# Interleaving the two token blocks in the matmul's stationary operands (xg, mixed, ff)

## The chip, the cores and the metric

The kernel runs on one core of one Trainium2 chip. The metric is the device time of one execution in microseconds (us), from the profiler's side of the device. Engines are named as in the profile: PE is TensorE (PEld is its weight load), DVE is VectorE, ACT is ScalarE, POOL is GpSimd, SP is SyncE. SP and ACT also issue DMAs (rows SPq and ACTq).

## The reference: one decoder layer

The layer has 256 tokens of width 2048, everything in float32. Cut to what matters:

```
h = rmsnorm(x, g_mix);  proj = h @ w_in            # all projections of two attentions and two gates
out_a = sparse attention with an indexer (top 64 keys); out_b = forgetting attention
mixed = sigmoid(gate_a) * (out_a @ w_o_a) + sigmoid(gate_b) * (out_b @ w_o_b)
x = x + mixed @ w_out
h = rmsnorm(x, g_ffn)
x = x + (silu(h @ w_ffn_gate) * (h @ w_ffn_up)) @ w_ffn_down      # width 5632
h = rmsnorm(x, g_ple)
x = x + sigmoid(h @ w_ple_gate) * (p @ w_ple_proj)
return rmsnorm(x, g_final)
```

## The kernel before

Every weight matrix is read once from HBM in chunks of 512 KB (128 partitions x 1024 float32) into `ws`, four slots in turn. ACT makes a rounded high part `hs` of each chunk (line 416), DVE the remainder `ls` (line 720). The activations are kept in high and low parts too, and a product is three matmuls: high x high, low x high, high x low.

Two forms of matmul stand in the program. In the first (lines 1165 and 1174) the weights are PE's stationary operand and the activations `hn` are streamed. In the second (`by_token`, lines 1275 and 1280) the activations are the stationary operand, a block of 128 rows (contraction) by 128 columns (tokens), and 512 columns of the weights are streamed. `pe.matmul(out, stationary, moving)` is the order of the arguments. A chunk holds two contraction tiles of 128 and is used for two blocks of tokens (b = 0: tokens 0 to 127, b = 1: tokens 128 to 255), so it takes eight matmuls with `hs` and four with `ls`. Which columns are the stationary block is said by `block_of(src, k, part, b)` (line 1264).

In the second half of the program, three products have activations that were made token by token and have to be turned first: `mixed` for w_out, `xg` for the FFN's gate and up matrices and for w_ple_gate, and `ff` for w_ffn_down. Turning 512 features of 256 tokens goes in four steps:

1. `turn_quads` (DVE, line 989): for each block b one transpose inside 32x32 squares, into `t_rows`;
2. `move_quads` (SP and ACT queues, line 224): sixteen DMAs, eight from each queue, carry squares between partitions, from `t_rows` into `t_cols`, with runs of 1 KB per partition;
3. ACT writes the high part from `t_cols` (`mixed_high` line 570, `new_high` line 598, `ff_hi` line 646);
4. DVE writes the low part (`mixed_low` line 994, `new_low` line 1023, `ff_low` line 1090).

Each engine works through its list in the written order and waits for semaphores. Of the 512-feature pieces, only the last of a stage is soon wanted: PE has started the next product with the earlier pieces and waits for `mix_ready` or `xg_ready` before it takes the last two chunks' tiles.

Of the kernel before, what the change touches and what calls it, by code (L numbers as in the profile page):

```python
# [3 lines left out]
F32 = mybir.dt.float32  # L4
F32R = mybir.dt.float32r
I32 = mybir.dt.int32
ALU = mybir.AluOpType
ACT = mybir.ActivationFunctionType
AX_X = mybir.AxisListType.X
ds = bass.ds  # L10

P = 128
D_MODEL, TOK, D_FF, D_PLE = 2048, 256, 5632, 256
# [4 lines left out]
KT = D_MODEL // P  # L18
KT_O = HA * HEAD // P
KT_FF = D_FF // P  # L20
# [52 lines left out]
QUAD = 32  # L73
QUADS = P // QUAD
# [38 lines left out]
def hybrid_layer(nc, c_rows, x, p, positions, g_mix, w_in, b_f, w_o_a, w_o_b, w_out, g_ffn, w_ffn_gate,  # L113
# [15 lines left out]
    def sb(name, kb, shape, dt=F32):  # L129
        return nc.alloc_sbuf_tensor_at(name, [P, *shape], dt, offset=base + int(kb * 1024))  # L130

    x_tok = sb("x_tok", 0, [2, D_MODEL])
    heads_o = sb("heads_o", 16, [KT, 2 * TOK], F32R)
    xg = sb("xg", 16, [2, KT, TOK], F32R)
    junk = sb("junk", 16, [2, D_MODEL])
    hn = sb("hn", 48, [KT, 2 * TOK], F32R)
    mixed = sb("mixed", 48, [2, KT, TOK], F32R)
    ff = sb("ff", 48, [2, KT_FF, TOK], F32R)
    gates = sb("gates", 80, [2, 2, D_MODEL])
    q_idx = sb("q_idx", 80, [KT_O, TOK])  # L140
    rope = sb("rope", 104, [4, 2 * TOK])
# [22 lines left out]
    mix_a = sb("mix_a", 188, [2, WIDE])  # L164
    silu_g = sb("silu_g", 188, [2, WIDE])
    sq = sb("sq", 188, [2, WIDE])
    t_cols = sb("t_cols", 184, [QUADS, 4, 2, QUAD])
    lg = sb("lg", 192, [CAT])
    pt = sb("pt", 193.5, [CAT])
    mask = sb("mask", 196.5, [CAT])  # L170
# [6 lines left out]
    k_st = sb("k_st", 200.5, [TOK])  # L177
    v_st = sb("v_st", 201.5, [2, P])
    p_cols = sb("p_cols", 192, [KT_PLE, 2 * TOK], F32R)
    t_rows = sb("t_rows", 196, [QUADS, 4, 2, QUAD])  # L180
    p_tok = sb("p_tok", 200, [2, D_PLE])
    ident = sb("ident", 202.5, [P])
    c_sum = sb("c_sum", 204, [TOK])
    gains = sb("gains", 205.5, [3 * KT])
# [25 lines left out]

    def by_tile(t):

        return t[:, :, :, :, :].rearrange("p a k b n -> p (k b) a n")

    def in_quads(t):

        return t.rearrange("p k (b a n) -> p (k b) a n", b=2, a=QUADS)

    def move_quads(eng, t, odd):

# [31 lines left out]
    merged, mix_s, mix_high, mix_ready = map(S, ("merged", "mix_s", "mix_high", "mix_ready"))  # L252
    x_new, x_sq, xg_high, xg_ready = map(S, ("x_new", "x_sq", "xg_high", "xg_ready"))
# [3 lines left out]
    ff_silu, ff_s, ff_high, ff_ready = map(S, ("ff_silu", "ff_s", "ff_high", "ff_ready"))  # L257
# [148 lines left out]
    def _(act):  # L406
# [37 lines left out]
        for t in range(KT // 2):  # L444
# [3 lines left out]
            for m in range(2):  # L448
                k = 2 * t + m
# [117 lines left out]

        def mixed_high(n):
            act.wait_ge(moved, 16 * MOVES * (T_MIX + n + 1))
            act.activation(in_quads(mixed[:, 0, 4 * n:4 * n + 4, :]), by_tile(t_cols), ACT.Copy).then_inc(mix_high, 1)  # L570

        act.wait_ge(gate_out, 2 * N_WIDE)
        for n in range(N_WIDE):
            cols = slice(WIDE * n, WIDE * (n + 1))
            if n == 0:
                split_chunks(C_WO + 4, 4)
            else:
                split_and_move(C_WO + 8 * n + 4, T_MIX + n - 1)
                mixed_high(n - 1)
            for gate in (1, 0):  # L580
                act.activation(gates[:, gate, :, cols], gates[:, gate, :, cols], ACT.Sigmoid).then_inc(gate_ready, 1)
            split_chunks(C_WO + 8 * n + 8, 4)
# [10 lines left out]
        def new_high(stage, n):  # L593

            act.wait_ge(moved, 16 * MOVES * ((T_X, T_PLE)[stage] + n + 1))
            for m in range(4):
                k = 4 * n + m
                act.activation(in_quads(xg[:, 0, k:k + 1, :]), by_tile(t_cols)[:, 2 * m:2 * m + 2], ACT.Copy,
                               scale=gains[:, KT * (stage + 1) + k:KT * (stage + 1) + k + 1]).then_inc(xg_high, 1)

        def root(stage):
# [3 lines left out]
        for n in range(N_WIDE):  # L605
            split_and_move(C_OUT + 8 * n + 4, T_MIX + N_WIDE - 1 + n)
            if n == 0:
                mixed_high(N_WIDE - 1)
                act.wait_ge(p_t, 1)
                act.activation(p_cols[:, :, 0:TOK], side[:, 2, :].rearrange("p (m n) -> p m n", m=2), ACT.Copy).then_inc(p_high, 1)  # L610
            else:
                squares(0, n - 1)
                new_high(0, n - 1)
            split_chunks(C_OUT + 8 * n + 8, 4)

        def ff_pair(i, step, first=False):

            u = U_FFN + 4 * step + i * 8
            c = step + i * 2
            split_high(u + 1, 0)  # L620
            split_high(u + 1, 1)
            move_quads(act, T_FF - 1 + c, 1)
            split_high(u + 1, 2)
            split_high(u + 1, 3)
            if first:
                squares(0, 3)
                new_high(0, 3)
                root(0)
            else:
                ff_hi(c - 1)  # L630
            for j in range(SLOTS):
                split_high(u + 2, j)
            if first:
                act.wait_ge(rms_ready, 1)
            for b in range(2):
                ins = act.activation(silu_g[:, b, :], acc[:, 2 + b, :], ACT.Silu, scale=rms[:, 0, 1, b:b + 1])
            ins.then_inc(ff_silu, 1)
            for j in range(SLOTS):
                split_high(u + 3, j)
            for j in range(SLOTS):  # L640
                split_high(u + 4, j)

        def ff_hi(c):

            act.wait_ge(moved, (c + T_FF + 1) * (16 * MOVES))
            act.activation(in_quads(ff[:, 0, ds(c * 4, 4), :]), by_tile(t_cols), ACT.Copy).then_inc(ff_high, 1)

        ff_pair(0, 0, first=True)
        with act.Fori(0, (N_FFN - 1) // 2) as i:
# [3 lines left out]
        for n in range(N_WIDE):  # L653
            at = C_DOWN + FF_CH * n
            split_and_move(at + 4, T_PLE - 1 + n)
            if n == 0:
                ff_hi(N_FFN - 1)
            else:
                squares(1, n - 1)
                new_high(1, n - 1)  # L660
            split_chunks(at + 8, FF_CH - 4)
# [24 lines left out]
        n = N_WIDE - 1  # L686
# [27 lines left out]
    def _(dve):  # L714
# [54 lines left out]
        for t in range(KT // 2):  # L769
# [3 lines left out]
            for m in range(2):  # L773
                k = 2 * t + m
# [125 lines left out]
        for i in range(4):  # L900
# [6 lines left out]
            if i % 2 == 1:  # L907
                n = i // 2
# [77 lines left out]
        def turn_quads(rows, at):  # L986

            for b in range(2):
                dve.transpose(t_rows[:, :, :, b, :].rearrange("p q k n -> p k q n"),
                              rows[:, b, at:at + WIDE].rearrange("p (k q n) -> p k q n", k=4, q=QUADS)).then_inc(turned, 1)  # L990

        def mixed_low(n):
            dve.wait_ge(mix_high, n + 1)
            dve.tensor_tensor(in_quads(mixed[:, 1, 4 * n:4 * n + 4, :]), by_tile(t_cols),  # L994
                              in_quads(mixed[:, 0, 4 * n:4 * n + 4, :].bitcast(F32)), ALU.subtract).then_inc(mix_ready, 1)

        for n in range(N_WIDE):
            cols = slice(WIDE * n, WIDE * (n + 1))
# [17 lines left out]
        def new_low(stage, n):  # L1016

            for m in range(4):
                k = 4 * n + m
                dve.wait_ge(xg_high, KT * stage + k // 2 * 2 + 2)  # L1020
                gain = gains[:, KT * (stage + 1) + k:KT * (stage + 1) + k + 1]
                for b in range(2):
                    ins = dve.scalar_tensor_tensor(in_quads(xg[:, 1, k:k + 1, :])[:, b], by_tile(t_cols)[:, 2 * m + b], gain,  # L1023
                                                   in_quads(xg[:, 0, k:k + 1, :].bitcast(F32))[:, b], ALU.mult, ALU.subtract)
                ins.then_inc(xg_ready, 1)

        def new_x(stage, n, pair):

            cols = slice(WIDE * n, WIDE * (n + 1))
            dve.tensor_tensor(x_tok[:, :, cols], acc[:, 2 * pair:2 * pair + 2, :], x_tok[:, :, cols], ALU.add).then_inc(x_new, 1)  # L1030
            dve.wait_ge(x_new, 4 * stage + n + 1)
            turn_quads(x_tok, WIDE * n)
# [22 lines left out]
        def ff_pair(i, step, first=False):  # L1055
# [5 lines left out]
            if first:  # L1061
                new_low(0, 3)
                row_sums(0)
                inverse(0)
                dve.wait_ge(rms_ready, 1)
            else:
                ff_low(c - 1)
# [15 lines left out]
            ins.then_inc(ff_s, 1)  # L1083
            dve.wait_ge(ff_s, c + 1)
            turn_quads(ff_tok, 0)

        def ff_low(c):

            dve.wait_ge(ff_high, c + 1)
            dve.tensor_tensor(in_quads(ff[:, 1, ds(c * 4, 4), :]), by_tile(t_cols),  # L1090
                              in_quads(ff[:, 0, ds(c * 4, 4), :].bitcast(F32)), ALU.subtract).then_inc(ff_ready, 1)

        ff_pair(0, 0, first=True)
        with dve.Fori(0, (N_FFN - 1) // 2) as i:
# [37 lines left out]
        n = N_WIDE - 1  # L1132
# [19 lines left out]
    def _(pe):  # L1152
# [105 lines left out]
        with pe.Fori(0, 4) as i:  # L1258
            for e in range(2):
                n = e + i * 2  # L1260
# [3 lines left out]
        def block_of(src, k, part, b):  # L1264

            if src is hn or src is heads_o or src is p_cols:
                return src[:, k, part * TOK + b * P:part * TOK + (b + 1) * P]
            return src[:, part, k, b * P:(b + 1) * P]

        def by_token(at, slot, tiles, src, banks, first, last, width=WIDE):  # L1270

# [100 lines left out]
        for n in range(N_WIDE):  # L1372
# [5 lines left out]
            for c in range(K_CH):  # L1378
                k = (KT_O + KW * c) % KT
# [112 lines left out]
```

## Time and profile before

| | |
|---|---|
| median of 3 executions | 1490.59 us (1490.31 to 1490.77) |
| the profiled execution's own time | 1490.77 us |
| its span, first to last instruction | 1489.0 us |
| PE busy | 1459.5 us, 98% |
| PE weight loads busy | 1222.0 us, 82% |
| DVE busy | 884.0 us, 59% |
| ACT busy | 690.6 us, 46% |
| POOL busy | 49.9 us, 3% |
| mean granted clock of PE | 0.997 of full speed |
| chain that ended last | PE 94%, DVE 3%, DMA 1% |

The rows further down are of a few views: the page of the profile, the list of waits, the list of instruction groups by line, the timeline (start, duration, engine, line, tile written <- tiles read, and in brackets the idle time before it with what ended it), and the chain that ended last. A matmul's record is longer than the distance to the next one, since matmuls are pipelined: the pace is read from the starts.

### The profile page before, as it was taken

Reading aid. Unit: us, or ns where it says so; the run is one execution under the profiler, and the core shown is the slowest. Engines: PE = TensorE matmul, PEld = TensorE weight load, DVE = VectorE, ACT = ScalarE, POOL = GpSimd, SP = SyncE. Lnnn points to the kernel's source line nnn. Section 1 sums busy time; section 2 is a strip of 40 time slices with the busy share of each in tenths; the row PEclk is TensorE's granted clock in tenths of the full one; section 3 lists DMA queues with packets and bytes.
Section 4 is the critical chain, followed back from the end, with each engine's and each line's share of the span. In section 5 each row is a group of like instructions: output and inputs, shape, how many; then the busy total and the mean of one; then the engine's idle time right before and its main releaser. Section 6 shows DMA issues by size and latency. Waiting matters only on the chain.

```text
span 1489.0 us, 19456 instructions
## 1 busy us (share of the span) xinstructions
PE 1459.5 (98%) x6841; PEld 1222.0 (82%) x6841; DVE 884.0 (59%) x1066; ACT 690.6 (46%) x846; POOL 49.9 (3%) x80
## 2 busy tenths in 40 slices
PE   5999999999999999999999999999999999999996
PEld 5888888888888888887888888888888888888885
DVE  6966776667655576665555555455555455554654
ACT  5644445544444455445444444444444343443544
POOL 0021001100111000000000000000000000000000
PEclk9999999999999999999999999999999999999998
DMA  6666565556655577666666666766666766666663
GB/s 193 178 204 169 160 222 170 169 170 190 183 166 167 163 236 232 211 208 214 205 209 210 202 191 205 212 207 210 205 204 184 221 204 197 210 190 209 213 215 109
DMA packets 182574, 290.91 MB, mean 195 GB/s; under 512 B 18745, under 2 KB 67825, under 8 KB 182001
## 3 DMA queue, kind: packets, MB, share of 16 engines
q1 hardware_dynamic: 172944, 281.02, 61.8%
q10 hardware_dynamic: 9568, 9.07, 2.1%
q8 instruction: 39, 0.64, 0.2%
q14 instruction: 23, 0.18, 0.0%
HBM read 275.87 MB, written 2.11 MB: 187 GB/s over the span
## 4 chain that ended last, share of the span: by engine, by line
PE 94%; DVE 3%; DMA 1%; ACT 1%; ACTq 1%; issue 0%; DVEq 0%
PE acc L1275 50%; PE acc L1280 25%; PE acc L1165 8%; PE acc L1174 4%; PE side L1275 2%; PE side L1280 1%; DVE ls L720 1%; ACTq L224 1%; DMA rope_c<-in_rope_rows 1%; PE side L1321 0%; DVE hn L775 0%; PE side L1327 0%; DMA t_cols<-t_rows 0%; ACT hs L416 0%; PE side L1335 0%
## 5 line engine op out<-in xcount | busy, mean ns | idle before, releaser
L720 DVE TENSOR_TENSOR ls<-ws,hs 128x1024 fp32r<-128x1024 f32 (+1 forms) x520 | 629.9, 1224 | 535.7 <-ACT hs L416 531.3
L416 ACT ACTIVATE hs<-ws 128x1024 fp32r<-128x1024 f32 (+1 forms) x520 | 544.1, 1056 | 717.8 <-PE acc L1280 505.0
L1275 PE MATMUL acc<-hs,xg 128*128 128x512 f32 x1648 | 407.1, 389 | 1.1 <-DVE xg L1023 1.1
L1275 PEld LDWEIGHTS acc<-hs,xg 128*128 128x128 f32 x1648 | 309.3, 188 | 65.6 <-DVE xg L1023 1.5
L1280 PE MATMUL acc<-ls,xg 128*128 128x512 f32 x824 | 220.2, 389 | 0.0
L1280 PEld LDWEIGHTS acc<-ls,xg 128*128 128x128 f32 x824 | 154.7, 188 | 32.1
L1275 PE MATMUL acc<-hs,ff 128*128 128x512 f32 x704 | 173.8, 389 | 0.0
L1275 PE MATMUL acc<-hs,hn 128*128 128x512 f32 (+1 forms) x704 | 171.9, 387 | 0.0
L1275 PEld LDWEIGHTS acc<-hs,ff 128*128 128x128 f32 x704 | 132.2, 188 | 27.4
L1275 PEld LDWEIGHTS acc<-hs,hn 128*128 128x128 f32 x704 | 127.1, 188 | 24.2
L1165 PE MATMUL acc<-hn,hs 128*128 128x512 f32 x560 | 139.2, 393 | 0.0
L1165 PEld LDWEIGHTS acc<-hn,hs 128*128 128x128 f32 x560 | 101.5, 189 | 18.9
L1280 PE MATMUL acc<-ls,ff 128*128 128x512 f32 x352 | 94.1, 389 | 0.0
L1280 PE MATMUL acc<-ls,hn 128*128 128x512 f32 (+1 forms) x352 | 90.4, 380 | 0.0
L1174 PEld LDWEIGHTS acc<-hn,ls 128*128 128x128 f32 x560 | 74.3, 191 | 5.1 <-DVE hn L775 0.7
L1280 PEld LDWEIGHTS acc<-ls,ff 128*128 128x128 f32 x352 | 66.1, 188 | 13.7
L1174 PE MATMUL acc<-hn,ls 128*128 128x256 f32 x560 | 75.9, 283 | 0.5 <-DVE hn L775 0.5
L1280 PEld LDWEIGHTS acc<-ls,hn 128*128 128x128 f32 x352 | 64.2, 188 | 13.1
L1275 PE MATMUL acc<-hs,mixed 128*128 128x512 f32 x256 | 63.5, 390 | 0.5 <-DVE mixed L994 0.5
L1275 PEld LDWEIGHTS acc<-hs,mixed 128*128 128x128 f32 x256 | 47.9, 188 | 10.9 <-DVE mixed L994 1.0
L533 ACT ACTIVATE lg<-lg,neg_max 128x128 f32<-128x128 f32 (+1 forms) x32 | 14.3, 448 | 47.0 <-DVE neg_max L935 47.0
L1280 PE MATMUL acc<-ls,mixed 128*128 128x512 f32 x128 | 34.2, 389 | 0.0
(192 smaller groups left out, 815.2 us busy)
## 6 DMA issues: line engine op xcount, KB each, us to landing
ws<-in_w_in SPq DMA_DIRECT2D x152, 512.0 KB, 3.9
ws<-in_w_ffn_gate SPq DMA_DIRECT2D x88, 512.0 KB, 4.4
ws<-in_w_ffn_up SPq DMA_DIRECT2D x88, 512.0 KB, 4.4
ws<-in_w_ffn_down SPq DMA_DIRECT2D x88, 512.0 KB, 4.3
ws<-in_w_out SPq DMA_DIRECT2D x32, 512.0 KB, 4.7
ws<-in_w_ple_gate SPq DMA_DIRECT2D x32, 512.0 KB, 3.9
ws<-in_w_o_b SPq DMA_DIRECT2D x16, 512.0 KB, 4.6
ws<-in_w_o_a SPq DMA_DIRECT2D x16, 512.0 KB, 4.6
```

The lines of the kernel that those rows point to most:

```text
L224: eng.dma_start(t_cols[QUAD * q:QUAD * (q + 1), a, :, :, :], t_rows[QUAD * a:QUAD * (a + 1), q, :, :, :]).then_inc(moved, 16)
L416: act.activation(hs[:, j, 0:n], ws[:, j, 0:n], ACT.Copy).then_inc(h_split, 1)
L533: act.activation(lg[:, cols], lg[:, cols], ACT.Exp, bias=neg_max[:, b:b + 1], accum_out=sums[:, b:b + 1]).then_inc(exp_done, 1)
L720: dve.tensor_tensor(ls[:, j, 0:n], ws[:, j, 0:n], hs[:, j, 0:n].bitcast(F32), ALU.subtract).then_inc(l_split, 1)
L1165: mm = pe.matmul(acc_of(bank + m, 2 * TOK), hs[:, j, at], src[:, k, :], start=first and q == 0, stop=last and q == len(tiles) - 1)
L1174: mm = pe.matmul(acc_of(bank + m, TOK), ls[:, j, at], src[:, k, 0:TOK], start=False, stop=False)
L1275: pe.matmul(banks[b], block_of(src, k, part, b), hs[:, slot, q * width:(q + 1) * width], start=first and q == 0 and part == 0, stop=False)
L1280: mm = pe.matmul(banks[b], block_of(src, k, 0, b), ls[:, slot, q * width:(q + 1) * width], start=False, stop=last and q == len(tiles) - 1)
```

## The change

The two token blocks are no longer one behind the other in the columns of `xg`, `mixed` and `ff`, but interleaved: column 2j holds token j, column 2j + 1 token 128 + j. To that end the transposes write `t_rows` with a step of two elements, `t_cols` has the block as its innermost index, ACT and DVE copy runs of 64 elements where they copied runs of 32, and the stationary block of a matmul is read with a step of two elements (8 bytes) where it was read in one run. `xg`'s low part, which took two DVE instructions per tile of 128 features, takes one. `hn`, `heads_o` and `p_cols` keep their layout.

```diff
-    xg = sb("xg", 16, [2, KT, TOK], F32R)
+    xg = sb("xg", 16, [KT, 2 * TOK], F32R)
     (mixed and ff likewise)
-    t_cols = sb("t_cols", 184, [QUADS, 4, 2, QUAD])
+    t_cols = sb("t_cols", 184, [QUADS, 4, QUAD, 2])
     (t_rows likewise)
     def by_tile(t):
-        return t[:, :, :, :, :].rearrange("p a k b n -> p (k b) a n")
+        return t[:, :, :, :, :].rearrange("p a k n b -> p k a (n b)")
     def in_quads(t):
-        return t.rearrange("p k (b a n) -> p (k b) a n", b=2, a=QUADS)
+        return t.rearrange("p k (a n) -> p k a n", a=QUADS)
     turn_quads:
             for b in range(2):
-                dve.transpose(t_rows[:, :, :, b, :].rearrange("p q k n -> p k q n"),
+                dve.transpose(t_rows[:, :, :, :, b].rearrange("p q k n -> p k q n"),
     new_high (mixed_high and ff_hi likewise):
-                act.activation(in_quads(xg[:, 0, k:k + 1, :]), by_tile(t_cols)[:, 2 * m:2 * m + 2], ACT.Copy,
+                act.activation(in_quads(xg[:, k:k + 1, 0:TOK]), by_tile(t_cols)[:, m:m + 1], ACT.Copy,
     new_low:
-                gain = gains[:, KT * (stage + 1) + k:KT * (stage + 1) + k + 1]
-                for b in range(2):
-                    ins = dve.scalar_tensor_tensor(in_quads(xg[:, 1, k:k + 1, :])[:, b], by_tile(t_cols)[:, 2 * m + b], gain,
-                                                   in_quads(xg[:, 0, k:k + 1, :].bitcast(F32))[:, b], ALU.mult, ALU.subtract)
-                ins.then_inc(xg_ready, 1)
+                dve.scalar_tensor_tensor(in_quads(xg[:, k:k + 1, TOK:2 * TOK]), by_tile(t_cols)[:, m:m + 1],
+                                         gains[:, KT * (stage + 1) + k:KT * (stage + 1) + k + 1],
+                                         in_quads(xg[:, k:k + 1, 0:TOK].bitcast(F32)), ALU.mult, ALU.subtract).then_inc(xg_ready, 1)
     block_of:
-            return src[:, part, k, b * P:(b + 1) * P]
+            return src[:, k, part * TOK:(part + 1) * TOK].rearrange("p (n b) -> p b n", b=2)[:, b, :]
```

On DVE, between the last piece of w_out's product and the FFN, stood in a row before (`x_tok` is the residual in token order, `xg` the turned and scaled one):

```order
L1030 TENSOR_TENSOR x_tok<-acc,x_tok 128x2x512
L989 STREAM_TRANSPOSE t_rows<-x_tok 128x4x4x32 x2
L720 TENSOR_TENSOR ls<-ws,hs 128x1024 x4
L1023 SCALAR_TENSOR_TENSOR xg<-t_cols,gains,xg 128x128 x8
L1036 TENSOR_REDUCE sum_sq<-parts_sq 128x2
L1040 RECIPROCAL rms<-rms 128x2
L720 TENSOR_TENSOR ls<-ws,hs 128x1024 x12
```

And now, at the same place of the same engine:

```order
L1028 TENSOR_TENSOR x_tok<-acc,x_tok 128x2x512
L989 STREAM_TRANSPOSE t_rows<-x_tok 128x4x4x32 x2
L720 TENSOR_TENSOR ls<-ws,hs 128x1024 x4
L1021 SCALAR_TENSOR_TENSOR xg<-t_cols,gains,xg 128x256 x4
L1034 TENSOR_REDUCE sum_sq<-parts_sq 128x2
L1038 RECIPROCAL rms<-rms 128x2
L720 TENSOR_TENSOR ls<-ws,hs 128x1024 x12
```

Eight instructions of 128 elements became four of 256; nothing else has another place. This stands eight times in the program. At the hand-over of `mixed` to w_out's product, the same engine's list shows another shape only:

```order
 L720 TENSOR_TENSOR ls<-ws,hs 128x1024 x4
-L994 TENSOR_TENSOR mixed<-t_cols,mixed 128x1024
+L994 TENSOR_TENSOR mixed<-t_cols,mixed 128x4x256
 L720 TENSOR_TENSOR ls<-ws,hs 128x1024 x4
 L1008 TENSOR_TENSOR mix_b<-acc,gates 128x1024
```

The number of elements is the same; what was one row of 1024 in eight parts is four parts of 256. PE, SP and POOL have the same instructions in the same order.

## Rows read from the trace of the kernel before

**Rows 1.** The page: busy time by engine, and the granted clock in 40 slices.
```profile
PE 1459.5 (98%) x6841; PEld 1222.0 (82%) x6841; DVE 884.0 (59%) x1066; ACT 690.6 (46%) x846; POOL 49.9 (3%) x80
PEclk9999999999999999999999999999999999999998
```

**Rows 2.** List of waits of PE: us in total, times, longest.
```profile
PE acc L1275 <- DVE xg L1023: 1.1, 1, 1.1
PE acc L1275 <- DVE mixed L994: 0.5, 1, 0.5
```

**Rows 3.** Groups by line: count | busy us, mean ns | idle before.
```profile
L1275 PE MATMUL acc<-hs,xg 128*128 128x512 f32 x1648 | 407.1, 389 | 1.1 <-DVE xg L1023 1.1
L1280 PE MATMUL acc<-ls,xg 128*128 128x512 f32 x824 | 220.2, 389 | 0.0
L1275 PE MATMUL acc<-hs,ff 128*128 128x512 f32 x704 | 173.8, 389 | 0.0
L1275 PE MATMUL acc<-hs,mixed 128*128 128x512 f32 x256 | 63.5, 390 | 0.5 <-DVE mixed L994 0.5
```

**Rows 4.** Timeline, FFN: one matmul and the load that begins beside it.
```profile
1100.09 0.39 PE L1275 MATMUL acc<-hs,xg 128*128 128x512 f32 x1
1100.10 0.19 PEld L1275 LDWEIGHTS acc<-hs,xg 128*128 128x128 f32 x1
```

**Rows 5.** The chain that ended last: start, us, what (pieces of 8 and 16).
```profile
1061.04 1.81 PE acc L1275 x8
1063.76 1.81 PE acc L1275 x8
368.05 1.91 PE acc L1174 x16
```

**Rows 6.** Timeline, attention: matmuls of 128 columns, two passes each.
```profile
240.03 0.38 PE L1334 MATMUL side<-pt,v_st 128*128 128x128 f32 x2
240.25 0.39 PE L1335 MATMUL side<-pt,v_st 128*128 128x128 f32 x2
```

**Rows 7.** Groups by line: two POOL copies of one shape.
```profile
L388 POOL COPY q_st<-q_cols 128x256 f32 x16 | 18.0, 1124 | 87.1 <-DVE k_cols L959 73.8 <-DVE k_cols L728 12.4
L389 POOL COPY k_st<-k_cols 128x256 f32 x16 | 7.3, 458 | 0.0
```

**Rows 8.** Groups by line: DVE work on chunks, and around the turning.
```profile
L720 DVE TENSOR_TENSOR ls<-ws,hs 128x1024 fp32r<-128x1024 f32 (+1 forms) x520 | 629.9, 1224 | 535.7 <-ACT hs L416 531.3 <-DVE sel L881 1.4 <-DVE q_idx L842 0.3
L1090 DVE TENSOR_TENSOR ff<-t_cols,ff 128x1024 f32 (+1 forms) x11 | 13.4, 1219 | 0.0
L989 DVE STREAM_TRANSPOSE t_rows<-x_tok 128x512 f32<-128x512 f32 x16 | 10.4, 691 | 0.3
L1023 DVE SCALAR_TENSOR_TENSOR xg<-t_cols,gains,xg 128x128 fp32r<-128x128 f32 x64 | 17.5, 348 | 8.3 <-ACT xg L598 8.3
L775 DVE SCALAR_TENSOR_TENSOR hn<-acc,gains,hn 128x256 fp32r<-128x256 f32 x8 | 3.4, 479 | 1.1 <-ACT hn L450 1.1
```

**Rows 9.** Timeline, the last piece of `mixed` on its way to PE.
```profile
577.43 1.31 DVE L989 STREAM_TRANSPOSE t_rows<-mix_b 128x512 f32<-128x512 f32 x2
578.77 5.30 ACTq L224 DMA_DIRECT2D t_cols<-t_rows  x8
587.54 1.22 DVE L994 TENSOR_TENSOR mixed<-t_cols,mixed 128x1024 fp32r<-128x1024 f32 x1
588.81 2.12 PE L1275 MATMUL acc<-hs,mixed 128*128 128x512 f32 x8 [0.55 <-DVE mixed L994]
```

**Rows 10.** Timeline, the last piece of `xg` on its way into the FFN.
```profile
663.42 1.31 DVE L989 STREAM_TRANSPOSE t_rows<-x_tok 128x512 f32<-128x512 f32 x2
665.40 6.16 ACTq L224 DMA_DIRECT2D t_cols<-t_rows  x8
676.03 2.19 DVE L1023 SCALAR_TENSOR_TENSOR xg<-t_cols,gains,xg 128x128 fp32r<-128x128 f32 x8 [0.92 <-ACT xg L598]
677.23 2.11 PE L1275 MATMUL acc<-hs,xg 128*128 128x512 f32 x8 [1.07 <-DVE xg L1023]
```

**Rows 11.** Timeline, the last piece of `xg` before w_ple_gate.
```profile
1394.99 2.19 DVE L1023 SCALAR_TENSOR_TENSOR xg<-t_cols,gains,xg 128x128 fp32r<-128x128 f32 x8 [1.31 <-ACT xg L598]
1398.16 1.98 PE L1275 MATMUL acc<-hs,xg 128*128 128x512 f32 x8
```

More of the change, by code:

```diff
@@ L133, in hybrid_layer @@
     heads_o = sb("heads_o", 16, [KT, 2 * TOK], F32R)
-    xg = sb("xg", 16, [2, KT, TOK], F32R)
+    xg = sb("xg", 16, [KT, 2 * TOK], F32R)
     junk = sb("junk", 16, [2, D_MODEL])
     hn = sb("hn", 48, [KT, 2 * TOK], F32R)
-    mixed = sb("mixed", 48, [2, KT, TOK], F32R)
-    ff = sb("ff", 48, [2, KT_FF, TOK], F32R)
+    mixed = sb("mixed", 48, [KT, 2 * TOK], F32R)
+    ff = sb("ff", 48, [KT_FF, 2 * TOK], F32R)
     gates = sb("gates", 80, [2, 2, D_MODEL])
@@ L179, in hybrid_layer @@
     p_cols = sb("p_cols", 192, [KT_PLE, 2 * TOK], F32R)
-    t_rows = sb("t_rows", 196, [QUADS, 4, 2, QUAD])
+    t_rows = sb("t_rows", 196, [QUADS, 4, QUAD, 2])
     p_tok = sb("p_tok", 200, [2, D_PLE])
@@ L569, in mixed_high @@
             act.wait_ge(moved, 16 * MOVES * (T_MIX + n + 1))
-            act.activation(in_quads(mixed[:, 0, 4 * n:4 * n + 4, :]), by_tile(t_cols), ACT.Copy).then_inc(mix_high, 1)
+            act.activation(in_quads(mixed[:, 4 * n:4 * n + 4, 0:TOK]), by_tile(t_cols), ACT.Copy).then_inc(mix_high, 1)
         act.wait_ge(gate_out, 2 * N_WIDE)
@@ L645, in ff_hi @@
             act.wait_ge(moved, (c + T_FF + 1) * (16 * MOVES))
-            act.activation(in_quads(ff[:, 0, ds(c * 4, 4), :]), by_tile(t_cols), ACT.Copy).then_inc(ff_high, 1)
+            act.activation(in_quads(ff[:, ds(c * 4, 4), 0:TOK]), by_tile(t_cols), ACT.Copy).then_inc(ff_high, 1)
         ff_pair(0, 0, first=True)
@@ L993, in mixed_low @@
             dve.wait_ge(mix_high, n + 1)
-            dve.tensor_tensor(in_quads(mixed[:, 1, 4 * n:4 * n + 4, :]), by_tile(t_cols),
-                              in_quads(mixed[:, 0, 4 * n:4 * n + 4, :].bitcast(F32)), ALU.subtract).then_inc(mix_ready, 1)
+            dve.tensor_tensor(in_quads(mixed[:, 4 * n:4 * n + 4, TOK:2 * TOK]), by_tile(t_cols),
+                              in_quads(mixed[:, 4 * n:4 * n + 4, 0:TOK].bitcast(F32)), ALU.subtract).then_inc(mix_ready, 1)
         for n in range(N_WIDE):
@@ L1089, in ff_low @@
             dve.wait_ge(ff_high, c + 1)
-            dve.tensor_tensor(in_quads(ff[:, 1, ds(c * 4, 4), :]), by_tile(t_cols),
-                              in_quads(ff[:, 0, ds(c * 4, 4), :].bitcast(F32)), ALU.subtract).then_inc(ff_ready, 1)
+            dve.tensor_tensor(in_quads(ff[:, ds(c * 4, 4), TOK:2 * TOK]), by_tile(t_cols),
+                              in_quads(ff[:, ds(c * 4, 4), 0:TOK].bitcast(F32)), ALU.subtract).then_inc(ff_ready, 1)
         ff_pair(0, 0, first=True)
```

## The prediction

> **What bounds the kernel now.** Read the page first: PE is busy 98% of the span, and the clock row stands at 9 to the last slice but one: the clock granted is the upper level, 2.4 GHz [rows 1]. DVE works 59% and ACT 46% of the span, so neither is short of time on the whole. The list of waits comes next. In the part of the program that the change touches PE waits twice in all, 1.1 us for `xg` and 0.5 us for `mixed` [rows 2]; everywhere else it goes from one matmul to the next. So the time is the number of matmuls times their pace, plus two short stalls, and the change can move the end in three ways only: by the pace of PE, by those two stalls, or by making a hand-over late that is in time now.
>
> How many matmuls read the changed layout: with `hs`, 1648 on xg, 704 on ff and 256 on mixed; with `ls` half as many each (824, 352, 128) [rows 3]; and 24 in the closing chunks by the code (2 blocks x 2 chunks x 2 tiles x 3). That is 2608 + 1304 + 24 = 3936 of PE's 6841.
>
> Their pace is read in the chain: two pieces of eight begin 2.72 us apart with a piece of four (line 1280) between them, so twelve matmuls take 2.72 us, 226.7 ns each [rows 5]. The streaming of 512 columns at 2.4 GHz is 213.3 ns of that. 3936 x 226.7 ns = 892 us: 60% of the time hangs on this one number.
>
> **PE: the stationary block is read with a step of two.** No instruction is added or taken away on PE. What differs is how a weight load reads its 128 columns: every second float32 instead of a run. The question is how much of the load is hidden now. One load begins together with the matmul before it, at 1100.10 beside 1100.09 [rows 4], and its matmul begins one pace later, so it has 226.7 ns. How long it needs at least is seen where the stream is short: the four passes of lines 1334 and 1335 with 128 columns begin 0.22 us apart for two, 110 ns per load and matmul, though 128 columns at 2.4 GHz are 53 ns [rows 6]; there the load sets the pace. With 256 columns the pace is 1.91 / 16 = 119 ns [rows 5]. The load's record of 190 ns is thus longer than its share of the pace; some 80 ns of it run beside the next load. A load needs 110 ns and has 227: it may take 2.06 times as long before the pace changes at all.
>
> No instruction of this trace reads a stationary block with a step, so the price has to be bounded. Lower end: nothing, and not below nothing, because the load is hidden already (what could be gained beyond is a rival below). Upper end: the widest spread that I find in this trace between two instructions of one shape is that of two POOL copies, 1124 against 458 ns, 2.45 times [rows 7]. A load that were 2.45 times as long would take 270 ns; the pace would go from 226.7 to 270, and 3936 x 43.3 ns = 170 us. I take nothing: it needs more than a doubling to be seen, and the nearest rows on patterns say that breaking a row up is free: DVE's reads and writes in runs of 32 elements take 1219 ns where the plain chunk takes 1224 [rows 8].
>
> The page "SBUF — State Buffer" of the Trainium skill (section Specifications) bears on this: memory lines of 16 bytes, and full bandwidth as long as at least two accesses fall into one line. A step of 8 bytes gives exactly two. By that rule the load stays at its present length; the trace before has no load with a step, so it neither agrees nor disagrees.
>
> **DVE: the transposes write with a step of two.** There are 46, of 691 ns each [rows 8]. They run while DVE has nothing urgent, except where the last piece of a stage is on its way to PE. For `mixed` the chain is transposes (577.43), the eight DMA issues on ACT's queue (578.77, 5.30 us), ACT's two chunks and its high part, DVE's low part (587.54), PE after 0.55 us of waiting [rows 9]. For `xg` into the FFN it is the same from 663.42 to PE's wait of 1.07 us at 677.23 [rows 10]. There each ns that two transposes take longer comes out at the end. In the third place, before w_ple_gate, the low part of the tiles that PE wants first is written by 1394.99 + 3 x 0.26 + 0.35 = 1396.1 and PE takes it at 1398.16: 2 us of slack [rows 11]. The other pieces are wanted many chunks later. Behind the transposes in DVE's list stand the `ls` chunks, for which PE has a lead: DVE idles 535.7 us before them in all, waiting for ACT [rows 8].
>
> Price: lower end nothing (the engine takes one element at a time, and the same number of them); upper end again 2.45 times, 691 x 1.45 = 1.0 us per transpose, two at each of two places, 4.0 us. I take nothing, by the same nearest rows.
>
> The page "Vector Engine (DVE) Microarchitecture Reference" (section Measured stream behaviour on trn2) speaks against the change here: it says that a DVE port keeps its full rate only while it finds at least two neighbouring words of 4 bytes together, and that a destination which jumps at every element takes 1.71 ns (2.5 for small steps) per column where 1.05 is normal. An estimate from it is 512 x 0.66 to 512 x 1.45 ns, 0.34 to 0.74 us per transpose, and 1.4 to 3.0 us for the two places. The row of 691 ns is of writes in runs and can't decide it.
>
> **DVE: one instruction for two in `xg`'s low part.** 64 of 128 elements become 32 of 256. Eight of the short ones take 2.19 us, the last 0.35 of it, so they follow at 0.26 us; the tiles that PE waits for are ready after four: 676.03 + 3 x 0.26 + 0.35 = 677.16, and PE starts at 677.23 [rows 10]. The nearest rows for the long form are those on `hn`, 479 ns, eight in 3.4 us or 0.425 each [rows 8]: two are ready after 0.425 + 0.48 = 0.90 us, at 676.93. That takes 0.25 us off PE's wait of 1.07; what is late next is ACT's high part, which ended a little before 676.03. At the other seven places the gain lies beside other work. Bounds: 0 to 0.5 us.
>
> **ACT's copies and DVE's other low parts** keep their element counts, with runs of 64 for runs of 32: nothing, from 1219 against 1224 ns [rows 8]. The DMAs still carry 1 KB runs, the same number in the same places.
>
> **The sum**, against the profiled execution's 1490.77 us (span 1489.0 and 1.8 around it): 0 for PE's loads, 0 for the transposes, - 0.25 for the low part of `xg`, so 1490.5. That execution was 0.2 above the median, so I forecast 1490.3 for a median. What a measurement of this kernel tells from no change is about 0.2%, 3.0 us.
>
> **The rivals.**
>
> *The load gets longer than its cover* (slower). Place: every one of the 3936 matmuls. It decides from 227 ns for a load, about twice the present 110. If the step just doubles the load to 220 ns and the 13 ns between the pace of 226.7 and the stream of 213.3 have to be paid on top, the pace is 233 and the cost 3936 x 6.6 ns = 26 us: 1516. At 2.45 times it is 170 us: 1661. For it: nobody in this trace reads with a step, and the product has 60% of the time under it, so that a small excess is multiplied at once. Against it: 117 ns of cover. Chances 5% for the first and 8% for the second.
>
> *The transposes slow down* (slower, small). Two at each of two hand-overs, decisive from the first ns. At 2.45 times + 4.0 us: 1494.3. With less, say half again, + 1.4 us: 1491.7. Chance of anything over 0.5 us 15%; in a third of that it is beyond 0.2%, which is 5%.
>
> *PE gets faster* (faster by over 0.2%). The 13 ns per matmul between pace and stream are not explained by the trace; if they came from the two operands' reads being in each other's way, another read pattern could free some. All of it would be 3936 x 13.4 ns = 53 us: 1438. Against it: the same 13 ns stand over 256 columns (119 - 107) [rows 5], so they look like a fixed hand-over. 0.2% needs 0.8 ns of it. Chance 4%.
>
> *Both waits of PE go*, because the hand-over is quicker than I take it: - 1.6 us, 1488.9, still within 0.2%. It belongs to "same".
>
> **How the numbers follow.** No change in PE's pace and transposes within 0.5 us: 68%, forecast 1490.3, own range 1489.5 to 1491.5. Transposes slower: 15% (10 within 0.2%, 5 beyond). Load beyond its cover: 13%. PE faster: 4%. So faster 0.04, within 0.2% 0.78, slower 0.18. The range goes from 1488.7, below which only a faster PE would take it, to 1496, which takes in the upper bound of the transposes; it leaves out both forms of the longer load and the faster PE, 17% together. The load's upper bound, 1661, stays outside.
>
> **What the changed profile would show.** Right: the pieces of twelve matmuls on xg, mixed and ff still 2.72 us apart, PEld's record still about 188 ns on them or at any rate below 227 + 80; transposes of 691 ns; 32 instructions of about 480 ns on line 1021; PE's wait for `xg` near 0.8 us and for `mixed` near 0.55. Wrong: a PEld record well over 300 ns and idle time or a wider pace on PE in every slice after the first third; or transposes over 900 ns with PE's two waits grown by twice the difference.

## The result, and the profile of the changed kernel

The changed kernel takes 1515.53 us (median of 4, 1515.39 to 1516.11) against 1490.62 us of the kernel before beside it: ratio 1.0168, 95% interval 1.015 to 1.0185. It is 25 us slower, outside the forecast range. The profiled execution took 1515.76 us with a span of 1513.9 us.

The page, busy time and granted clock: the same count of matmuls at the same clock, busy 26 us longer; DVE has 32 instructions less and is 5 us less busy (compare [rows 1]).

```profile
PE 1485.6 (98%) x6841; PEld 1251.8 (83%) x6841; DVE 879.3 (58%) x1034; ACT 691.0 (46%) x846; POOL 49.9 (3%) x80
PEclk9999999999999999999999999999999999999999
```

List of waits of PE, the rows that answer to [rows 2]: the wait for `mixed` is as before, the one for `xg` is gone, and none is new.

```profile
PE acc L1273 <- DVE mixed L994: 0.5, 1, 0.5
```

Groups by line (count | busy, mean ns of one | idle before). The three tiles with the new layout have longer matmul records (395 for 389 in [rows 3]) and loads of 195 and 196 ns; the same line on `hn` and `heads_o`, whose layout is untouched, stays at its old 387 and 390 with loads of 188.

```profile
L1273 PE MATMUL acc<-hs,xg 128*128 128x512 f32 x1648 | 418.1, 395 | 0.0
L1273 PEld LDWEIGHTS acc<-hs,xg 128*128 128x128 f32 x1648 | 322.1, 195 | 62.6 <-DVE xg L1021 0.3
L1273 PE MATMUL acc<-hs,ff 128*128 128x512 f32 x704 | 178.6, 396 | 0.0
L1273 PEld LDWEIGHTS acc<-hs,ff 128*128 128x128 f32 x704 | 138.0, 196 | 26.3
L1273 PE MATMUL acc<-hs,hn 128*128 128x512 f32 (+1 forms) x704 | 171.9, 387 | 0.0
L1273 PEld LDWEIGHTS acc<-hs,hn 128*128 128x128 f32 x704 | 127.1, 188 | 24.2
L1273 PE MATMUL acc<-hs,heads_o 128*128 128x512 f32 x128 | 31.7, 390 | 0.0
```

The chain that ended last (start, us, what), in the FFN:

```profile
1060.03 1.87 PE acc L1273 x8
1061.90 0.93 PE acc L1278 x4
1062.83 1.87 PE acc L1273 x8
```

Twelve matmuls take 2.80 us where they took 2.72 [rows 5]: 233.3 ns each instead of 226.7. 3936 x 6.67 ns = 26.2 us, less the 1.1 us of the wait that went, is 25.1; the spans differ by 24.9. The whole result is in the pace.

What DVE does around the turning (groups by line), and the last piece of `xg` on its way into the FFN (timeline):

```profile
L989 DVE STREAM_TRANSPOSE t_rows<-x_tok 128x512 f32<-128x512 f32 x16 | 10.5, 693 | 0.3
L1021 DVE SCALAR_TENSOR_TENSOR xg<-t_cols,gains,xg 128x256 fp32r<-128x256 f32 x32 | 13.5, 482 | 10.5 <-ACT xg L598 10.5
L1088 DVE TENSOR_TENSOR ff<-t_cols,ff 128x1024 f32 (+1 forms) x11 | 13.5, 1225 | 11.9 <-ACT ff L646 11.9
```

```profile
677.08 1.71 ACT L598 ACTIVATE xg<-t_cols,gains 128x256 fp32r<-128x256 f32 x4
678.02 1.68 DVE L1021 SCALAR_TENSOR_TENSOR xg<-t_cols,gains,xg 128x256 fp32r<-128x256 f32 x4 [0.85 <-ACT xg L598]
678.95 1.02 PEld L1273 LDWEIGHTS acc<-hs,xg 128*128 128x128 f32 x5 [0.28 <-DVE xg L1021]
678.96 1.21 PE L1273 MATMUL acc<-hs,xg 128*128 128x512 f32 x4
```

The transposes with their step-2 writes take 693 ns, 2 more than in [rows 8]. The long form on `xg` takes 482 ns. The first load on the new tiles is let go by DVE at 678.95 and its matmul starts 0.94 us after DVE began, where it was 1.20 in [rows 10]; PE itself shows no idle time there, since the matmuls before it fill the time up to about 678.94. The 11.9 us that DVE idles before `ff` have no row in PE's list of waits.

### The profile page after: what moved, and what is told of

Its sections match the earlier page's. It is cut to its first block, busy times and chain, and to the rows that moved or that the text cites. A ratio compares the mean times of both kernels' runs of the same rounds, so it can differ in the third digit from the quotient of the medians.

```text
span 1513.9 us, 19424 instructions
## 1 busy us (share of the span) xinstructions
PE 1485.6 (98%) x6841; PEld 1251.8 (83%) x6841; DVE 879.3 (58%) x1034; ACT 691.0 (46%) x846; POOL 49.9 (3%) x80
## 4 chain that ended last, share of the span: by engine, by line
PE 94%; DVE 3%; DMA 1%; ACT 1%; ACTq 1%; issue 0%; DVEq 0%
PE acc L1273 51%; PE acc L1278 25%; PE acc L1163 8%; PE acc L1172 4%; PE side L1273 2%; PE side L1278 1%; DVE ls L720 1%; ACTq L224 1%; DMA rope_c<-in_rope_rows 1%; PE side L1319 0%; DVE hn L775 0%; DMA ws<-in_w_out 0%; PE side L1325 0%; ACT hs L416 0%; PE side L1333 0%
## 5 line engine op out<-in xcount | busy, mean ns | idle before, releaser
L1273 PE MATMUL acc<-hs,xg 128*128 128x512 f32 x1648 | 418.1, 395 | 0.0
L1273 PEld LDWEIGHTS acc<-hs,xg 128*128 128x128 f32 x1648 | 322.1, 195 | 62.6 <-DVE xg L1021 0.3
L1278 PE MATMUL acc<-ls,xg 128*128 128x512 f32 x824 | 225.7, 395 | 0.0
L1278 PEld LDWEIGHTS acc<-ls,xg 128*128 128x128 f32 x824 | 161.1, 195 | 31.2
L1273 PE MATMUL acc<-hs,ff 128*128 128x512 f32 x704 | 178.6, 396 | 0.0
L1273 PEld LDWEIGHTS acc<-hs,ff 128*128 128x128 f32 x704 | 138.0, 196 | 26.3
```

What stands on the lines that cost most here:

```text
L1273: pe.matmul(banks[b], block_of(src, k, part, b), hs[:, slot, q * width:(q + 1) * width], start=first and q == 0 and part == 0, stop=False)
L1278: mm = pe.matmul(banks[b], block_of(src, k, 0, b), ls[:, slot, q * width:(q + 1) * width], start=False, stop=last and q == len(tiles) - 1)
```

## The experiments

Two theories at first. A: PE's read of the stationary block with a step costs the time. B: it is the new place of the data, or how DVE and ACT write them. Each was put alone.

**e1: the changed kernel, blocks read in one run.**

```diff
-            return src[:, k, part * TOK:(part + 1) * TOK].rearrange("p (n b) -> p b n", b=2)[:, b, :]
+            return src[:, k, part * TOK + b * P:part * TOK + (b + 1) * P]
```

> The changed kernel with the stationary blocks of xg, mixed and ff read in one run of 128 columns again (so a block holds the wrong tokens); transposes, copies and the single low-part instruction stay as changed. Theory A (the step in PE's stationary read costs the time, 3936 matmuls at 233.3 instead of 226.7 ns): the pace is back at 226.7 ns, 1490.3 us, within 0.5 us of the kernel before. Theory B (the cost lies in where the data sit or in how DVE and ACT write them, for example the new addresses of high and low parts): the pace stays near 233.3 ns and the time near 1515.5.

Measured: 1490.65 us, ratio 1.0002 (0.9992 to 1.0011). The chain shows the old pace:

```profile
1060.22 1.81 PE acc L1273 x8
1062.04 0.91 PE acc L1278 x4
1062.94 1.81 PE acc L1273 x8
```

**e2: the kernel before, blocks read with a step of two.**

```diff
-            return src[:, part, k, b * P:(b + 1) * P]
+            return src[:, part, k, :].rearrange("p (n b) -> p b n", b=2)[:, b, :]
```

> The kernel before with one edit: the stationary blocks of xg, mixed and ff are read with a step of two columns out of the old layout (so a block holds the wrong tokens). Theory A: 1490.6 + 3936 x 6.7 ns = 1516.9 us, pace 233.3 ns. Theory B: 1490.6 us, pace 226.7 ns.

Measured: 1515.82 us, ratio 1.0171 (1.0154 to 1.0188), which is the changed kernel's time. Groups by line:

```profile
L1275 PE MATMUL acc<-hs,xg 128*128 128x512 f32 x1648 | 417.8, 394 | 0.2 <-DVE xg L1023 0.2
L1275 PEld LDWEIGHTS acc<-hs,xg 128*128 128x128 f32 x1648 | 318.3, 193 | 66.7 <-DVE xg L1023 0.7
```

A holds and B falls: one line of the change carries all of it, and the rest of the change together costs nothing that can be measured. With plain blocks (e1) PE's wait for `xg` is gone as well, and the one for `mixed` is 1.1 us.

**e4: the paces by themselves.** A kernel of runs of 96 matmuls, fp32r (the type of the high and low parts), with the two operands each taken from two places in turn:

```
for i in range(96):
    pe.matmul(bank, stat[:, at:at + (cols - 1) * step + 1:step], mov[:, m0:m0 + (n - 1) * mstep + 1:mstep], ...)
```

> Nothing of the layer is computed: after a load of x only runs of 96 matmuls each, one kind per line, all fp32r. Read is the pace of each kind. Step 1 with 512 columns: 226.7 ns = 213.3 + 13.3 by all theories, step 2: 233.3. They part at step 4 and on. Lines theory (the stream pauses for each new 16-byte line that the load touches: 32 lines at step 1, 64 at step 2, 128 from step 4 on; + 6.7 ns per 32 lines): step 3 240, step 4 and 8 and 16 all 247 ns; a block of 64 columns at step 1 223 ns, 32 columns 222. Fixed theory (any step other than one costs the same): 233.3 at all steps. Duration theory (the load itself takes longer and outlasts its cover): records of the loads grow with the pace, and with 256 columns the step-2 pace grows by far more than 6.7 ns, to 220 or so if the load had doubled. A step of two in the moving operand: fixed and lines theory leave open what it does; if the moving stream too needs its line only once per 4 columns, the pace rises there as well.

Measured (mean distance between the 96 starts, which the trace has to 1 ns; median record of a load; 128 columns in the block unless said). The bare kernels e4, e7 and e9 were each executed once; the plain kind comes out at 226.7 in all three:

| block | stream | pace ns | load ns |
|---|---|---|---|
| step 1 | 512 | 226.7 | 188 |
| step 2 | 512 | 233.3 | 193 |
| step 3 | 512 | 235.5 | 253 |
| step 4 | 512 | 235.0 | 310 |
| step 8 | 512 | 245.3 | 331 |
| step 16 | 512 | 235.3 | 300 |
| step 1, start at word 1 | 512 | 232.4 | 188 |
| step 1 | 256 | 120.0 | 192 |
| step 2 | 256 | 120.0 | 195 |
| step 4 | 256 | 233.3 | 329 |
| step 1, 64 columns | 512 | 230.0 | 134 |
| step 1 | 512 with step 2 | 453.1 | 207 |

The rows of some of them (records min/median/max in ns, then first and last start in us; the pace is the distance of the two over 95, and the tenths of a us shown here leave it open by about 1 ns): line 65 is step 1, 68 step 2, 74 step 4, 98 step 2 under 256 columns, and 101 step 4 under 256 columns.

```profile
L65 PE MATMUL acc<-mov,stat x96: 388/389/392, 42.0 to 63.5; 128*128 128x512 f32 x96
L68 PE MATMUL acc<-mov,stat x96: 393/394/397, 63.8 to 85.9; 128*128 128x512 f32 x96
L74 PE MATMUL acc<-mov,stat x96: 393/399/402, 108.8 to 131.1; 128*128 128x512 f32 x96
L98 PE MATMUL acc<-mov,stat x96: 278/283/286, 278.4 to 289.8; 128*128 128x256 f32 x96
L101 PE MATMUL acc<-mov,stat x96: 393/396/400, 289.9 to 312.1; 128*128 128x256 f32 x96
```

```profile
L68 PEld LDWEIGHTS acc<-mov,stat x96: 193/193/194, 63.5 to 85.7; 128*128 128x128 f32 x96
L74 PEld LDWEIGHTS acc<-mov,stat x96: 307/310/312, 108.5 to 130.9; 128*128 128x128 f32 x96
```

Three things follow. A load with step 2 needs no more than 120 ns: under 256 columns the pace is 120.0 with either step. A load with step 4 needs twice that: 233.3 under 256 columns, and in e7 232.9 under 384, so there the load sets the pace. That is over the 226.7 of a plain pair, and under 512 columns the pace is 235.0: all but 1.7 ns of this is the load's own length. And a price of the size of step 2's stands where there is neither a step nor a longer load, with a start at word 1 or with a shorter block. So none of the three theories written down for this run holds: not lines (step 4 should have been 247, 64 columns 223), not a fixed price for a step, not duration.

**e5 and e6: two of these in the full kernel.** For e5 the blocks are plain but start at an odd word; for e6 they are read with a step of four.

```diff
-            return src[:, part, k, b * P:(b + 1) * P]
+            return src[:, part, k, 1 + 126 * b:129 + 126 * b]                      # e5
+            at = k // 2 * 2                                                         # e6
+            return src[:, part, at:at + 2, :].rearrange("p k n -> p (k n)").rearrange("p (n s) -> p s n", s=4)[:, 2 * (k % 2) + b, :]
```

> The kernel before with one edit: the stationary blocks of xg, mixed and ff are one run of 128 columns as ever, but begin at an odd word (columns 1 to 128 and 127 to 254, so a few tokens are wrong). Step theory (only a step in the read costs): 226.7 ns and 1490.3 us. Disturbance theory (226.7 ns is the pace of a load that is one run AND begins on the boundary of a memory line; whatever else costs 4 to 9 ns under a stream of 512 columns): the pace of the bare run of this kind, 232.4 ns, so 1490.3 + 3936 x 5.7 ns = 1512.8 us.

> The kernel before with one edit: the stationary blocks of xg, mixed and ff are read with a step of four columns out of two neighbouring tiles (so they hold wrong tokens and features). The bare runs gave 235.0 ns for it, and 233.3 ns with a stream of 256 columns, where the load itself sets the pace. Cover theory (a load that has doubled is still covered by a stream of 512 columns, and pays the small disturbance only): 235.0 ns, 1490.3 + 3936 x 8.3 = 1523.1 us. Duration theory (cost grows with the load's own time, from 120 to 233 ns): far more than step 2, at the very least twice its 25 us, 1540 us or over.

Here the two blocks of e5 begin at word 1 and at word 127 in turn. Measured: e5 1511.78 us, ratio 1.014 (1.0124 to 1.0157); e6 1523.17 us, 1.0223 (1.0205 to 1.0241). Groups by line, e5 first:

```profile
L1275 PE MATMUL acc<-hs,xg 128*128 128x512 f32 x1648 | 414.8, 394 | 0.5 <-DVE xg L1023 0.5
L1275 PEld LDWEIGHTS acc<-hs,xg 128*128 128x128 f32 x1648 | 309.3, 188 | 74.1 <-DVE xg L1023 1.0
```

```profile
L1276 PE MATMUL acc<-hs,xg 128*128 128x512 f32 x1648 | 421.3, 398 | 0.2 <-DVE xg L1023 0.2
L1276 PEld LDWEIGHTS acc<-hs,xg 128*128 128x128 f32 x1648 | 402.0, 310 | 0.7 <-DVE xg L1023 0.5
```

In e5 the loads are those of the kernel before to the nanosecond, 188, and the time is 21 us longer: something is paid that is not the length of the load. In e6 the loads' records are 122 ns longer and the time 32 us. This run does not tell the two causes apart. By the bare runs the load alone needs 233.3 ns, 6.6 more than the plain pace, which is 26 of the 32 us; what falls is only the duration theory as it was written down, with 1540 us or more. Both forecasts from bare paces were met within 1.1 us, but for e5 that is luck in part: it took the pace of start 1 (232.4) for both blocks, and e9 found 226.7 for start 127 by itself. With that for half of the matmuls the sum is 1501.5, 10 us less than measured. A block at 127 is thus not free when it takes turns with one at word 1. That the pace needs some ten matmuls to settle (last section), while the blocks change every two or four, would fit, but it is not shown.

**e8: is it those three tiles?** The blocks of `hn`, `heads_o` and `p_cols` with the step of two, the others plain.

```diff
-                return src[:, k, part * TOK + b * P:part * TOK + (b + 1) * P]
+                return src[:, k, part * TOK:(part + 1) * TOK].rearrange("p (n b) -> p b n", b=2)[:, b, :]
```

> The kernel before with xg, mixed and ff read plainly and instead hn, heads_o and p_cols read with a step of two in by_token (wrong tokens in those blocks). If the price belongs to the read and not to those tiles, 960 + 384 + 48 = 1392 matmuls with a stream of 512 columns pay 6.7 ns each and the 96 with a stream of 256 nothing: + 9.3 us, 1499.6 us. If the price had to do with xg, mixed and ff alone, 1490.3.

Measured: 1499.82 us, ratio 1.006 (1.0043 to 1.0076). The price goes with the read, whatever the tile. That the sum came out within 0.3 us hides a spread: the matmuls' records grow by 6 ns on `hn` (397 to 403 at 512 columns) and by 8 to 9 on `heads_o` (389 and 390 to 398), and why `heads_o` pays more is open.

**e7 and e9: starts and lengths, bare.** Both are e4 with starts for each operand as well.

> Again bare runs of 96 matmuls each, nothing of the layer. First starts of the stationary block at 0, 1, 2, 3, 4, 8, 16, 32 words. Line theory (a load that begins inside a 16-byte line touches 33 lines and falls out of rhythm): 226.7 ns at 0, 4, 8, 16, 32 and 230 to 233 at 1, 2, 3. Then starts of the moving operand at 1, 2, 4, 16 words: if the two reads meet in the same memory and it is their distance that counts, an odd start there costs alike, and odd starts on both sides cost nothing; if only the load's own alignment counts, 226.7 whatever the moving start. Then step 2 with other starts (233.3 throughout if it is the step alone), both operands at one address, and streams of 320, 384, 448, 480, 496 columns at step 1 and 2: the point at which step 2 begins to cost. Cover theory: the load needs 120 ns, so with 320 columns (133 + 13) step 2 costs what it costs at 512 or nothing, never more. Last, blocks of 96 and 120 columns.

> Bare runs of 96 matmuls each once more, nothing of the layer. The sweeps before showed 226.7 ns only where the load is one run of 128 columns and both operands start at a multiple of 128 words; a stationary start at 4 to 32 words paid 6 to 7 ns, a moving start at 16 words 2 ns. Boundary theory (the good pace needs both starts on a boundary of some size up to 512 bytes, each for itself): 226.7 at starts 128, 256, 512, 1024 on either side, more at 64 and 96 on the stationary side, and equal odd distances on both sides (4, 16, 32, 64 words) do not heal it. Distance theory (the two reads meet in the same memory, and what counts is how far apart they are): equal starts on both sides give 226.7 again. For step 2: 233.3 whatever the moving start by the boundary theory; some moving start brings it back to 226.7 by the distance theory. With a stream of 384 columns all starts give 173.3 by the cover theory (there was no price for step 2 there). The last kind is the plain one again and has to return to 226.7 if a rhythm does not outlive its cause.

Measured, step 1 and 512 columns unless said, starts in words of 4 bytes, pace in ns:

| stationary start | 0, 64, 256, 512, 1024 | 127 | 128 | 1 | 2 | 3 | 4, 8, 16 | 32, 96 |
|---|---|---|---|---|---|---|---|---|
| pace | 226.7 | 226.7 | 227.0 | 232.4 | 230.7 | 233.3 | 233.3, 233.4, 233.4 | 232.5 |

| moving start | 64 | 128, 256, 512 | 1 | 2 | 4 | 16 | 32 |
|---|---|---|---|---|---|---|---|
| pace | 226.8 | 226.7 | 236.5 | 233.2 | 231.7 | 228.9 | 233.3 |

| both starts equal | 1 | 4 | 16 | 32 | 64 |
|---|---|---|---|---|---|
| pace | 237.8 | 230.0 | 226.7 | 227.1 | 226.7 |

| columns streamed | 320 | 384 | 448 | 480 | 496 |
|---|---|---|---|---|---|
| step 1 | 146.6 | 173.4 | 202.7 | 216.9 | 220.0 |
| step 2 | 146.6 | 173.3 | 203.4 | 216.6 | 225.3 |

Step 2 with moving starts 1, 16, 64, 128, 256 or stationary starts 1, 4, 64, 128: 233.2 to 233.4 every time; with moving start 2 it is 235.0. Plain blocks of 96 and 120 columns: 230.0 and 233.3. From e9, line 83 has the moving operand at word 32, line 104 both at 32, line 110 the stationary one at 127, line 119 step 2 with the moving one at 128. From e7, line 89 has the moving operand at word 1, and line 155 is step 4 under 384 columns. Loads on line 68 of e7, with a start at word 1, still take 187 to 188 ns.

```profile
L83 PE MATMUL acc<-mov,stat x96: 387/394/399, 172.2 to 194.3; 128*128 128x512 f32 x96
L104 PE MATMUL acc<-mov,stat x96: 387/389/398, 325.4 to 347.0; 128*128 128x512 f32 x96
L110 PE MATMUL acc<-mov,stat x96: 388/389/396, 369.0 to 390.6; 128*128 128x512 f32 x96
L119 PE MATMUL acc<-mov,stat x96: 393/394/395, 435.6 to 457.7; 128*128 128x512 f32 x96
```

```profile
L89 PE MATMUL acc<-mov,stat x96: 389/398/401, 220.2 to 242.7; 128*128 128x512 f32 x96
L155 PE MATMUL acc<-mov,stat x96: 341/394/407, 673.2 to 695.3; 128*128 128x384 f32 x96
```

The boundary theory falls: 16, 32 and 64 on both sides give the good pace back, though 16 and 32 on the stationary side alone cost 6 to 7 ns. So the distance between the two starts counts, and every distance that is a multiple of 64 words was good where the starts were multiples of 16; 32 and 96 cost the same. The theory of the 16-byte line falls with starts 4, 8 and 16. Distance is not the whole rule either: equal starts at 1 and 4 words don't heal, and a stationary start at 127 (226.7) and a moving start at 1 (236.5) both put the stationary read one word short of a multiple of 64 from the moving one, with 10 ns between them. Nor does every start off a multiple of 16 cost, as 127 shows. The full rule is open. For step 2 none of the distances tried helps. Under 384 columns step 2 costs nothing, but starts at 16 and 1 (174.7, 175.0) and a moving start at 1 (178.4) cost 1 to 5 ns, against what was expected. The last plain run is back at 226.7.

**e11 and e10: the distance of 64 words, and a repaired version, in the full kernel.** For e11 the block is always columns 64 to 191. For e10 the changed kernel gets plain blocks and keeps the one instruction per tile: the two blocks stay interleaved in `t_rows` and `t_cols` only.

```diff
-            return src[:, part, k, b * P:(b + 1) * P]                               # e11
+            return src[:, part, k, 64:64 + P]
-    t_cols = sb("t_cols", 184, [QUADS, 4, QUAD, 2])                                 # e10
+    t_cols = sb("t_cols", 184, [4, QUADS, QUAD, 2])
     by_tile:  "p a k n b -> p k a (n b)"  becomes  "p k a n b -> p k b (a n)"
     in_quads: "p k (a n) -> p k a n"      becomes  "p k (b n) -> p k b n", b=2
     move_quads writes t_cols[QUAD * q:QUAD * (q + 1), :, a, :, :]; block_of as in e1
```

> The kernel before with one edit: the stationary block of xg, mixed and ff is always columns 64 to 191, one run of 128 (both blocks hold the same, partly wrong tokens). The distance of the two reads is then an odd multiple of 64 words. By the bare runs (226.67 ns at 64 words, 232.4 at 1 and 96, all with the same length of load) the pace stays at 226.7 and the time at 1490.3 us, where the odd start had cost 21 us. If any start other than a multiple of 128 words costs in the full kernel, 1512.

> A version of the changed kernel that computes the reference: the interleaving stays in t_rows and t_cols only (t_cols with the tile as its outermost index), ACT and DVE undo it while they write the high and low parts, so that the stationary blocks are runs of 128 columns again and xg's low part is still one instruction per tile. The DMAs into t_cols now land in four runs of 256 bytes instead of one of 1 KB. Theory (the whole loss is PE's read of the block): pace 226.7 ns, time within 0.2% of the kernel before, 1490.3 plus or minus 3 us; PE's two short waits may move by tenths of a us in either direction with the DMAs. Rival (the smaller runs delay the hand-overs): the two waits grow by a us or more each.

Measured: e11 1490.6 us, ratio 0.9999 (0.999 to 1.0009). e10 1491.0 us, ratio 1.0004 (0.9995 to 1.0013). Groups and waits of e10:

```profile
L1273 PE MATMUL acc<-hs,xg 128*128 128x512 f32 x1648 | 407.1, 389 | 0.1
L1273 PEld LDWEIGHTS acc<-hs,xg 128*128 128x128 f32 x1648 | 309.2, 188 | 64.7 <-DVE xg L1021 0.5
```

```profile
PE acc L1273 <- DVE mixed L994: 1.1, 1, 1.1
```

The pace is back, the wait for `xg` is down to 0.1 us and that for `mixed` up to 1.1. The smaller runs of the DMAs are not shown to be the reason for the latter, since e1 has the same 1.1 with runs of 1 KB. The repaired version is 24.5 us faster than the changed kernel and equal to the kernel before within what can be measured: the rest of the change is harmless, and its gain is too small to see.

## Why the prediction was wrong

*What bounds the kernel*: right. 3936 matmuls times their pace carried the whole result, 24.9 us of span.

*PE's stationary read*: wrong, and this is the step that failed: "it may take 2.06 times as long before the pace changes at all". I took the 227 ns that a load has and the 110 that it needs as a slack in which nothing can happen. As far as the load's own length goes that was right: a load with step 2 needs no more than 120 ns (the pace under 256 columns, with either step), and one with step 4, which needs 233.3, comes to 235.0 under 512 columns, little more than its own length. But beside its length a load has another way to cost. With the length unchanged, the pace of a plain block moved between 226.7 and 237.8 ns with the starts of the two operands alone, and it went up by 6.7 ns with a step of two. The term that I set at 0 measured 6.7 ns x 3936. What inside the chip makes the pace depend on the two reads, no run shows.

*The first rival* had almost the time, 1516, for a wrong reason: it let the load double to 220 ns. The load's record grew from 188 to 193 or 196 and its need stayed within 120 ns. A load that really doubles is that of e6, and it gives 1523. What was right in it is the sentence that the product has 60% of the time under it, so that a small excess is multiplied at once; 5% was far too little for that. The bounds were built for a load that outlasts its cover, and had nothing for one that costs while it is covered. Two signs that the pace was more than the stream stood in the trace: the 13 ns between them, which I noted as unexplained, and the 224 to 236 ns after a change of shape (below). Whether they have the same cause as the 6.7 ns is open.

*Transposes with step-2 writes*: right, 693 ns. The page "Vector Engine (DVE) Microarchitecture Reference" of the Trainium skill (Measured stream behaviour on trn2), which asks for pairs of neighbouring words, does not hold for this step: the trace shows 2 ns more, not 340 to 740. The 16-byte rule of "SBUF — State Buffer" (Specifications) agrees with the loads' records, 188 and 193 ns for steps 1 and 2, 253 for 3, 310 for 4; that section says nothing of two reads at once, and the pace went by more than the loads' records: 233.3 ns with a load of 193 and 233.4 with one of 188. For the moving operand the rule does not hold: with a step of two it streams at half the rate (453.1 ns).

*One low-part instruction for two*: right in size. 482 ns against 479 assumed; the tiles are ready 0.26 us sooner, where 0.25 was said.

*The remaining wait*: the wait for `xg` was to shrink to 0.8 us and went altogether. A later PE is not the whole reason, for in e1, at the old pace, it went too. It also moves from profile to profile where nothing near it was changed (0.4 us in e11, 0.6 in e8, 1.1 in the kernel before), so one profile of each kernel can't settle tenths of a us here.

## What to carry to other kernels

An engine that is busy 98% of the time is sensitive to what its hidden work does to it, not only to whether that work ends in time: before a layout change under a long stream of matmuls, measure the pace of exactly that pair of reads in a bare run, in the order in which the kernel takes its blocks. That foretold e6, e8 and e11 within 0.3 us; e5, whose blocks took turns in a way that no bare run had, was met by luck in part. The good pace was found only with a stationary fp32r block in one run of 128 columns; of the starts tried, those were safe that are multiples of 16 words on both sides and a multiple of 64 words apart. Interleave in the staging buffers instead, where steps of two cost DVE 2 ns in 691 and ACT 85 in 1046.

## What the runs showed that I had not expected

The pace is a rhythm that has to be found. In the timeline of the kernel before, the eight matmuls after a change of shape (227.99) are followed 1.93 us later by the next piece, those at 230.84 after 1.81. The first distance is 314 ns, and the next eight lie between 224 and 236:

```profile
227.99 2.10 PE L1275 MATMUL acc<-hs,hn 128*128 128x512 f32 x8
229.92 1.08 PE L1280 MATMUL acc<-ls,hn 128*128 128x512 f32 x4
230.84 1.98 PE L1275 MATMUL acc<-hs,hn 128*128 128x512 f32 x8
232.65 1.07 PE L1280 MATMUL acc<-ls,hn 128*128 128x512 f32 x4
```

A plain load too pays for some ten matmuls after a change to 512 columns from a shorter stream, and then locks at 226.7. Under 256 columns nothing of the kind is seen: at 371.64 the pace stands at 120 from the second matmul on. With a step of two the changed kernel does not come down: its mean stays at 233.3, with distances of 229 and 237 ns in turn. That the two reads meet in parts of the memory that repeat every 64 words would fit most of the starts (not 127), but it is an inference: no run looks inside, and why 13.3 ns are left at best, why a block of 64, 96 or 120 columns (230.0, 230.0, 233.3) is slower than one of 128, and why step 2 costs under 1 ns up to 480 columns and then 5 to 7 stays open. Blocks in several runs, say four of 32, were not tried.

A moving operand with a step of two is dear: 453.1 ns for 512 columns, twice the plain pace. And ACT minds what DVE does not: in e10 it reads `t_cols` with a step of two and takes 1131 ns for 1024 elements instead of 1046, while DVE's instruction on the same data stays at 1217.
